# First and last expert rows on SyncE's queue, and the next layer's norm inside the embedding's loop

## What is computed

```python
for i in range(2):
    a = rms_norm(h, norm_mix[i])
    h = h + mixer_i(a)
    h = h + hier_moe(rms_norm(h, norm_ffn[i]))        # 32 experts, top 2
    gate = sigmoid(rms_norm(h, ple_norm[i]) @ ple_w_gate[i] + ple_b_gate[i])
    h = h + gate * (p[i] @ ple_w_proj[i])             # the embedding
```

## Time and profile before

| | before |
|---|---|
| median of 3 runs | 3158.64 us (3158.44 to 3161.94) |
| the profiled execution's own time | 3159.78 us |
| its span, first to last instruction | 3158.2 us |
| PE busy | 92% of the span |
| mean granted TensorE clock | 0.959 |

### The profile page before, as it was taken

How to read it: one execution, slowest core, us unless ns; L and a number is a source line. 1 busy time by engine, 2 the same in 40 slices (tenths; PEclk the granted TensorE clock), 3 DMA queues, 4 the chain that set the end, 5 groups by cost and what they waited for, 6 DMA issues and landing times. The chain is left out here.

```text
span 3158.2 us, 32607 instructions
## 1 busy us (share of the span) xinstructions
PE 2916.5 (92%) x12473; PEld 1569.3 (50%) x12474; DVE 1128.2 (36%) x2460; ACT 652.6 (21%) x1258; POOL 243.5 (8%) x352
## 2 busy tenths in 40 slices
PE   7999899999799999979979899877997999999798
PEld 5544555555444444424467644477654444444243
DVE  2585355544300000005364635566563000000052
ACT  3310355521100010103021124322211010100030
POOL 0000000001100000011000000043201000000110
PEclk9999999999799999989989899988997999999899
DMA  4000791031599999964020110000416999999630
GB/s 157 27 27 0 309 384 54 1 116 67 214 419 417 413 404 403 390 249 170 40 78 1 16 68 27 0 2 23 161 54 238 410 421 414 406 405 394 247 150 40
DMA packets 138547, 617.21 MB, mean 195 GB/s; under 512 B 25188, under 2 KB 31748, under 8 KB 121992
## 3 DMA queue, kind: packets, MB, share of 16 engines
q1 hardware_dynamic: 110952, 525.93, 42.3%
q0 software_dynamic: 24064, 86.00, 7.2%
q10 hardware_dynamic: 3376, 3.19, 0.3%
HBM read 508.00 MB, written 105.91 MB: 194 GB/s over the span
## 5 line engine op out<-in xcount | busy, mean ns | idle before, releaser
L1994 PE MATMUL acc<-wg,xt 128*128 128x512 f32 x512 | 223.6, 600 | 0.0
L2590 PE MATMUL acc<-xt,work 128*128 128x512 f32 x384 | 166.9, 593 | 0.0
L757 PE MATMUL acc<-h,xt 128*128 128x512 f32 x384 | 165.2, 592 | 0.0
L1994 PEld LDWEIGHTS acc<-wg,xt 128*128 128x128 f32 x512 | 98.6, 193 | 123.7 <-issue 123.7
L396 PE MATMUL scores<-qkt 65*128 65x512 f32 (+7 forms) x384 | 147.9, 495 | 0.9 <-DVE qkt L536 0.9
L542 DVE TENSOR_REDUCE nmax<-scores 128x1 f32<-128x256 f32 (+7 forms) x128 | 96.8, 756 | 76.5 <-PE scores L398 74.4
L1740 PE MATMUL py<-place 128*64 128x512 f32 (+1 forms) x352 | 120.2, 595 | 1.0 <-DVE place L1820 1.0
L1740 PE MATMUL pu<-place 128*128 128x512 f32 (+1 forms) x320 | 119.8, 593 | 0.0
L757 PEld LDWEIGHTS acc<-h,xt 128*128 128x128 f32 x384 | 72.9, 190 | 91.1 <-issue 90.9
L2590 PEld LDWEIGHTS acc<-xt,work 128*128 128x128 f32 x384 | 72.0, 190 | 86.1 <-issue 86.1
L1263 PE MATMUL acc<-place 128*128 128x512 f32 x256 | 112.7, 594 | 1.1 <-PEq L64 1.1
(11 more groups left out here) (638 smaller groups left out, 5145.0 us busy)
## 6 DMA issues: line engine op xcount, KB each, us to landing
own<-in_moe_w_gate_dram SPq DMA_DIRECT2D x22, 2048.0 KB, 16.7
place<-in_moe_w_down_dram SPq DMA_DIRECT2D x22, 2048.0 KB, 16.3
place<-in_moe_w_up_dram SPq DMA_DIRECT2D x20, 2048.0 KB, 17.8
slots_out<-zeros SPq DMA_DIRECT2D x4, 9216.0 KB, 62.9
place<-in_moe_w_gate_dram SPq DMA_DIRECT2D x18, 2048.0 KB, 20.9
own<-in_moe_w_up_dram SPq DMA_DIRECT2D x16, 2048.0 KB, 16.1
own<-in_moe_w_down_dram SPq DMA_DIRECT2D x10, 2048.0 KB, 19.4
xt<-in_moe_w_gate_dram SPq DMA_DIRECT2D x9, 2048.0 KB, 23.0
```

The source lines that it names most:

```text
L757: last = pe.matmul(acc[:, n % 4, 0:width], xs[:, k, tile_of(i)], weights[:, k, cols], start=(k == 0), stop=(k == k_of - 1))
L1994: last = pe.matmul(acc[:, u % 4, :], xt[:, k, i * P:(i + 1) * P], wg[:, k, n * SLAB:(n + 1) * SLAB], start=(k == 0), stop=(k == KD - 1))
L2590: last = pe.matmul(acc[:, n % 4, :], slabs[m // 4 % 2][:, k, (m % 4) * P:(m % 4 + 1) * P], xt[:, k, half * SLAB:(half + 1) * SLAB], start= ...
```

## The change

It has three parts. First, the loads of the first two units' rows go from POOL's queue to SP's, behind the wait for `scattered`, with semaphores of their own (`first_in`). Second, the last unit's rows are written by SP, which waits for them (`last_out`); POOL's last writes are now those of the unit before. Third, `rmsnorm_transpose` is gone. `layer_embedding` in layer 0 takes the next layer's gain and does its norm by tiles: PE turns tile i-2 behind unit (i, 0), ACT and DVE square, root, scale and copy a half of each turned tile. `xt` and `s5_t` are allocated outside for this, and half of the gather's row buffers lie in `s5_t`.

```diff
@@ mixer_end, SP
                 bring_in(nc, sp, own_loads, z["own_in"])
+                sp.wait_ge(c.scattered, (layer + 1) * 16 * 2 * NT)
+                for n in range(2):
+                    sp.dma_start(m[:, n, :], c.slots_in[units[n][0] * REGION:units[n][0] * REGION + P, :]).then_inc(c.first_in[n], 16)
@@ mixer_end, POOL
-                pool.wait_ge(c.scattered, (layer + 1) * 16 * 2 * NT)
-                for n in range(2):
-                    pool.dma_start(m[:, n, :], c.slots_in[units[n][0] * REGION:units[n][0] * REGION + P, :]).then_inc(c.x_in[n], 16)
@@ first_blocks, SP, behind the last weights
+                n = UNITS - 1
+                rows = P // len(units[n])
+                sp.wait_ge(y_act, n + 1)
+                sp.wait_ge(y_dve, n + 1)
+                for a, q in enumerate(units[n]):
+                    sp.dma_start(c.slots_out[bass.ds(expert[q] * P, rows), :], y[a * rows:(a + 1) * rows, n % 2]).then_inc(last_out, 16)
+                sp.wait_ge(last_out, 16 * len(units[n]))
@@ first_blocks, POOL
-                rows_out(UNITS - 1)
-                for n in (UNITS - 2, UNITS - 1):
+                for n in (UNITS - 3, UNITS - 2):
                     pool.wait_ge(y_out[n % 2], y_before[n % 2] + 16 * arrivals[n])
@@ first_blocks, PE, turn(n)
-                    pe.wait_ge(x_in[n % 2], x_before[n % 2] + 16 * arrivals[n])
+                    if n < 2:
+                        pe.wait_ge(c.first_in[n], 16 * (layer + 1))
...
@@ layer_embedding, SP
+                if next_gain is not None:
+                    sp.wait_ge(combined, NT)
+                    sp.dma_start(next_gains, row(next_gain).to_broadcast([P, D])).then_inc(next_gain_in, 16)
...
@@ layer_embedding, PE, behind each unit
                     last.then_inc(multiplied, 1)
+                    if next_gain is not None and n == 0 and i >= 2:
+                        next_turn(i - 2)
+                if next_gain is not None:
+                    next_turn(NT - 2)
+                    next_turn(NT - 1)
@@ layer_embedding, ACT
                     act.activation(gate[:, u % 3, :], gate[:, u % 3, :], ACT.Sigmoid).then_inc(gated, 1)
+                    if next_gain is not None:
+                        if u % 2 == 0 and u >= 2:
+                            next_square(u // 2 - 1)
+                        if u % 2 and u >= 5:
+                            next_copy((u - 5) // 2)
+                        if u % 2 and u >= 3:
+                            next_root((u - 3) // 2)
+                if next_gain is not None:
+                    next_square(NT - 1)
+                    next_root(NT - 1)
+                    next_copy(NT - 2)
+                    next_copy(NT - 1)
@@ layer_embedding, DVE
+                    if next_gain is not None and u % 2:
+                        if u >= 5:
+                            next_copy((u - 5) // 2)
+                        if u >= 3:
+                            next_scale((u - 3) // 2)
                 add(UNITS - 1)
+                if next_gain is not None:
+                    next_scale(NT - 1)
+                    next_copy(NT - 2)
+                    next_copy(NT - 1)
@@ odd_mixer
-        rmsnorm_transpose(nc, c, h, t["norm_mix"][layer], h, xt,
-                          loads=[(early[:, :, 0:half], slab_of(w_in, OD_G, half))])
```

More of the change, by code:

```diff
@@ L153, in _ @@
             pool.tensor_copy(c.causal16[:], c.causal[:])
[L156 to L251, removed]
@@ L1124, in constants @@
     c.x_in = [ctx.enter_context(nc.semaphore(f"x_in{n}")) for n in range(2)]
+    c.first_in = [ctx.enter_context(nc.semaphore(f"first_in{n}_{next(NUMBER)}")) for n in range(2)]
     c.y_out = [ctx.enter_context(nc.semaphore(f"y_out{n}")) for n in range(2)]
@@ L1891, in moe, with layer_embedding @@
     overflow_blocks(nc, c, t, layer, r, ring, m)
-def layer_embedding(nc, c, t, h, layer, r, out_dram):
+def layer_embedding(nc, c, t, h, layer, r, out_dram, xt, later, next_gain=None, loads=()):
     KE = 256 // P
     with ExitStack() as ctx:
-        xt = sbuf(nc, ctx, "xt", [P, KD, S])
         wp = sbuf(nc, ctx, "wp", [P, KE, D])
@@ L1906, in layer_embedding @@
         normed = sbuf(nc, ctx, "normed", [P, 2, D])
-        rows = sbuf(nc, ctx, "rows", [P, 4, 2, D])
+        own_rows = sbuf(nc, ctx, "own_rows", [P, 2, 2, D])
+        rows = [own_rows[:, 0], own_rows[:, 1]] + [later.rearrange("p k n -> p (k n)").rearrange("p (a b d) -> p a b d", a=2, b=2)[:, n] for n in range(2)]
+        next_normed, next_gains = own_rows[:, 0], own_rows[:, 1, 0]
+        next_ms, next_rms, next_rstd = [sbuf(nc, ctx, n, [P, NT]) for n in ("next_ms", "next_rms", "next_rstd")]
         proj = sbuf(nc, ctx, "proj", [P, NT, D])
@@ L1936, in _ @@
                     sp.dma_start(bias[:], row(t["ple_b_gate"][layer]).to_broadcast([P, D])).then_inc(bias_in, 16)
+                if next_gain is not None:
+                    sp.wait_ge(combined, NT)
+                    sp.dma_start(next_gains, row(next_gain).to_broadcast([P, D])).then_inc(next_gain_in, 16)
+                    with nc.allow_non_contiguous_dma(reason="weights' column slabs"):
+                        for tile, view in loads:
+                            sp.dma_start(tile, view).then_inc(loaded, 16)
                 for i in range(NT):
@@ L1940, in _ @@
                 sp.wait_ge(h_out, 16 * NT)
+                if loads:
+                    sp.wait_ge(loaded, 16 * len(loads))
             @block.gpsimd
@@ L1960, in turn, with next_turn @@
                     last.then_inc(turns, 1)
+                def next_turn(i):
+                    pe.wait_ge(next_scaled, i + 1)
+                    if i >= 2:
+                        pe.wait_ge(next_act, i - 1)
+                        pe.wait_ge(next_dve, i - 1)
+                    for k in range(KD):
+                        last = pe.transpose(turned[i % 2][:, k * P:(k + 1) * P], next_normed[:, i % 2, k * P:(k + 1) * P], c.ident[:])
+                    last.then_inc(next_turns, 1)
                 pe.wait_ge(p_in, 16)
@@ L3140, with odd_mixer @@
     pass
-def odd_mixer(nc, c, t, h, layer, r):
+def odd_mixer(nc, c, t, h, layer, r, xt, s5_t):
     j = layer // 2
```

66 lines of the change are left out of this document (49 added, 17 removed).

## The result

The changed kernel takes 3133.98 us (median of 4 runs, 3133.13 to 3135.87), the kernel before 3159.95 (4 runs, 3158.44 to 3161.94). The ratio is 0.9918, with a 95% interval of 0.9901 to 0.9935. The profiled execution took 3134.64 us.

What follows compares the result with a forecast made beforehand. PE, busy 92% of the span, can gain only where it stands still, at the ends of stages. 6.0 + 9.0 + 13.0 - 0.6 = 27.4 us off 3158.64 gives 3131.2, range 3127 to 3139.

Steps and rivals of the forecast that it cites:

- first rows: Start of the experts: with SP loading the first rows, PE starts 3.1 and 2.9 us earlier; 6.0 us in all.
- last rows: End of the experts: with SP writing the last rows, the embedding starts 4.5 us earlier per layer; 9.0 us in all.
- norm: Norm by tiles inside the embedding: 30.7 us removed, a 12.5 us tail and 5.2 us of transposes added; gain 13.0.
- clears at the end: End of the span: the embedding's 36 semaphores for 26 leave more clears exposed, a loss of 0.6 us.
- step about the DRAIN: Before the experts: POOL's DRAIN starts at 825.4 behind the last scatter and ends at 830.5, before SP arrives at 831.05.
- low case: First rows: if the DRAIN lasted until 5.1 us behind the scatters' landing, PE would start at 833.9; sum 1.9 us.
- The DRAIN's length: POOL's DRAIN at block ends: at least 5.1 us from its own start, longer only while transfers are under way.
- The low end of the range: Whole kernel: all high ends together (6.6, 9.8, 14, and 1 from the clock) give 3127 us.
- The pages: Two skill rules: ACT table switches drain about 1.38 us more (whole 3132.6); issuing from several queues saves only issue time.
- Rival 1: Experts' ends: changing the queue moves the wait without shortening it, saving only issue time; 14.8 us, 3143.8; chance 0.06.
- Rival 2: Embedding: PE waits for the next norm in each tile; a chain of 8 us gives 3138; chance 0.08 beyond 3139.
- Rival 3: Embedding: norm tiles slip a unit, PE stands 5 us six times and loses its clock; slower, 3173 us; chance 0.03.

Runs made afterwards that it cites:

- e1: The kernel before with only the experts' first rows moved from POOL's queue to SP's; 3154.35 us, ratio 0.9984.
- e2: The kernel before with only the experts' last rows moved from POOL's queue to SP's; 3152.42 us, ratio 0.9974.
- e3: The changed kernel with first and last rows put back on POOL's queue, leaving only the norm by tiles; 3146.14 us, ratio 0.9956.
- e8: The changed kernel with SP clearing early, the last rows' landing awaited at the embedding's head, and 26 semaphores in layer 1's embedding; 3121.93 us.
- e10: e8 with the clears of the experts' and the overflow stage's semaphores put off to SP's idle time in the embedding; 3120.67 us, ratio 0.9885.
- e9: The changed kernel with POOL also waiting for the scatters' landing at the end of the stage before the experts; 3133.18 us, ratio 0.9920.
- e5: The changed kernel with SP clearing the previous stage's 37 semaphores before its wait for the last rows' halves; 3127.67 us, ratio 0.9899.
- e7: The changed kernel with an extra root and sigmoid on ACT ahead of each root of the next norm; 3145.57 us, ratio 0.9956.
- e12: The kernel of e9 with one direct 64-byte transfer by POOL as its last act in the stage, waited for; one execution took 3137.58 us.

## Why the prediction was right, step by step

The time came at 3134.0 for 3131.2, inside 3127 to 3139. Against the profiled executions the sum was 27.4, and 25.1 came.

| term | predicted | changed kernel | by itself |
|---|---|---|---|
| first rows | 6.0 | 3.00 + 2.65 = 5.7 | e1: 5.6 at the place |
| last rows | 9.0 | 3.80 + 3.91 = 7.7 | e2: 7.8 at the place |
| norm | 13.0 | 30.74 - 12.40 - 5.5 = 12.8 | e3: 13.1 at the place |
| clears at the end | -0.6 | -0.9 | e8 and e10 have 26 again |

These give 25.3; drifts of a few tenths of us in other stages make up the rest. One of them has a cause that I see: the stage behind the norm takes 7.27 us for 6.80 to its next transposes, because it starts at the low clock (granted 0.50, which is 1.2 GHz, until 1591.8, where the kernel before had 1.00 in the same products), 0.5 of the 1 us that the prediction allowed.

- *First rows.* Step and size held: PE waits for rows that landed 3.2 us after SP's issue, where 2.9 was taken. The step about the DRAIN was right only in what it was needed for. It was to start at 825.4 and end at 830.5; it started at 823.9 and ended at 829.6, 0.7 us behind the scatters' landing (SP woke at about 828.9). That the two ends lie near each other is luck: by the count of 16 alone it would have taken 1.4 us, and it was the landing that held it. The low case, a DRAIN of 5.1 behind that landing, was made in e9 and took 1.37: it could not have happened.
- *Last rows.* This is the term that was mis-sized, 7.7 for 9.0. SP had both halves issued 1.5 us behind DVE's copy (issues of 0.48 and 0.59, with register work between them) where 0.6 was taken, so 4.9 us went to the landing and not 4.3. The 37 clears took 2.5 and not 2.1 us: 0.068 each, where rows 5 gave 0.057. The handoff behind them took 2.5 for 2.95, and gave 0.4 back. That is 0.6 + 0.4 - 0.4 = 0.6 us in each layer, so SP's issue is the largest part. The issue and the clears both run on SP; e5 shows it for the clears, whose 2.5 us come back in full when they are moved, and no run changed SP's issue.
- *The DRAIN's length.* "At least 5.1 us from its own start" was the wrong reading of rows 4. It costs 0.08 us for each of POOL's transfers in the block. The number came out because the experts have 62 of them; the cover, which I put at 6 us, was thick enough for 4.96 to vanish.
- *The norm.* The chain was to be 5.0 and is 4.87; its reserve was to be 1.9 us and is 1.8; the tail was to be 12.5 and is 12.40; six tiles were to cost 5.2 and cost 5.5. e7 spent the reserve and PE stood 1.1 us at a tile, where 3.0 - 1.8 = 1.2 was the excess.
- *The low end of the range.* Its terms, with the 0.6 of clears taken off as in the sum, give 3158.64 - 30.8 = 3127.8; the 3127 leaves that term out. The measured time lies far from that end.
- *The pages.* On ACT's table switches the rows of the tail show a load of 1.28 us from 1577.32 and the root at 1578.61, 0.01 behind its end. By the Trainium skill's ScalarE: Activation LUTs (What ACT_TABLE_LOAD costs) a drain of about 1.38 us would lie beside each switch; the trace doesn't show one. As to queues, e2 measures 7.8 us for moving two transfers. The Trainium skill's Trainium Kernel Development and Optimization (Key Constraints), by which another queue saves issue time alone, would make it 2.4 us, an estimate from POOL's two issues (1.2 us a layer). The trace disagrees, because the queue's engine also pays at the end of the block.

Rival 1 is refuted by e1 (5.6 us where it had none) and e2 (7.8 where it had 2.4). Rival 2 didn't come about, and its price was too low: e7 made its chain of 8 us and the median rose by 11.6, where 6.6 was said. Rival 3 is not settled. e7's stands of 1.1 us left the clock alone, but rival 3 has stands of 5, and the one stand of that length here, in the tail, was followed by transposes at 1.97 us. A chain of 11.5 us, from which it was to make the kernel slower, was not tried; since the tail was left out of its price too, the point at which the gain is gone lies at a shorter chain.

## What to carry to other kernels

When a stage ends on a barrier, list what each engine does between its last useful instruction and that barrier (DRAINs, semaphore clears, waits for landings) and move it under the last long piece of work of another engine; here 37 clears (2.5 us) were worth nearly as much as the landing of half a megabyte (3.1). A row that names a cost does not say what the cost grows with: change the count and the kind apart before the number is used elsewhere. For work that is put into another stage, compute the reserve of its chain against the unit that covers it; what goes beyond it is paid at every tile, and in the tail the whole of the added chain is paid once for each of the last tiles (here 3.0 us twice).

## What the runs showed of the hardware

- A DRAIN of POOL at a block's end took 1.37, 1.46, 4.96 and 5.12 us for 16, 17, 60 and 62 transfers issued by POOL in the block, all landed, some long before; with none 0.05. That is 0.08 to 0.09 us for each, the same for an indirect scatter of 144 packets (e9) and a direct transfer of 64 bytes in 32 packets (e12). A block with direct transfers alone and as few as 16 was not tried.
- A semaphore's clear by SP took 0.057 to 0.068 us from start to start: 37 in 2.5 us, 21 in 1.1, 36 in 2.3.
- The last rows took 3.0 to 3.2 us to land by SP where POOL's took 2.9 to 3.6; the queue's gain was not in the transfer there. The first load of rows took 3.2 us by SP and 3.7 by POOL.
- In e7, PE stood 1.1 us every 16 us and kept the upper clock (transposes at 1.09 us); each such stand made the period 1.3 us longer. The stand of 5.0 us in the changed kernel's tail was followed by transposes at 1.97.
